# Two transformer blocks: seams between stages reordered, and a final sum shared between VectorE and TensorE

## The reference

```
h = modulate(rmsnorm(x), shift2, scale2)
group = top1 of softmax(h @ rg_w + rg_b)                # 4 groups
e_p, e_idx = top2 of softmax(h @ re_w + re_b)[group]    # 8 experts in a group
weights = g_p * e_p / sum(e_p)
y[token] += weight * ((silu(h @ w_gate[e]) * (h @ w_up[e])) @ w_down[e])
out = rmsnorm(x + gate2 * y, final_norm_g)
```

## Time and profile before

| | us |
|---|---|
| median of 3 runs | 3078.43 (3071.15 to 3080.0) |
| profiled execution | 3087.37 |
| its span, first to last instruction | 3085.6 |
| TensorE busy | 2895.9 (94%) |
| VectorE busy | 1779.8 (58%) |
| ScalarE busy | 1094.2 (35%) |
| mean granted TensorE clock | 0.970 |
| expert stage, its start to the next one's | 685.1 |
| last stage | 52.6 |

### The profile page before, as it was taken

One profiled execution on the slowest core, in us unless ns is written; L12 is line 12 of the kernel. 1 busy time (PEld: TensorE's weight loads), 2 busy tenths in 40 slices (PEclk: granted clock), 3 DMA queues, 4 the chain that ended last, 5 costly groups with the idle time before them and its releaser, 6 DMA issues. The chain is left out here.

```text
span 3085.6 us, 47695 instructions
## 1 busy us (share of the span) xinstructions
PE 2895.9 (94%) x19486; PEld 2179.9 (71%) x19486; DVE 1779.8 (58%) x2743; ACT 1094.2 (35%) x1700; POOL 454.5 (15%) x352
## 2 busy tenths in 40 slices
PE   8999999999999999989999999998898999999991
PEld 6877644676777777767747768687688777777760
DVE  3332222485566666555434626253874899999984
ACT  2111100122455454452231313222531566665652
POOL 2222100021322222213131101010000000000001
PEclk9999999999999999999999999998898999999995
DMA  4111031663222112121221211016346899999975
GB/s 167 45 38 45 15 129 55 184 194 123 61 61 63 55 55 62 56 100 51 68 56 34 65 29 60 7 59 202 129 166 224 329 396 397 398 398 398 397 286 231
DMA packets 290940, 454.44 MB, mean 147 GB/s; under 512 B 15760, under 2 KB 157584, under 8 KB 290752
## 3 DMA queue, kind: packets, MB, share of 16 engines
q1 hardware_dynamic: 283696, 426.06, 39.6%
q0 software_dynamic: 7056, 25.69, 2.1%
HBM read 389.77 MB, written 61.93 MB: 146 GB/s over the span
## 5 line engine op out<-in xcount | busy, mean ns | idle before, releaser
L1016 PE MATMUL psum<-x_hi,w_hi 128*128 128x512 f32 x512 | 210.6, 411 | 2.3 <-PEq L100 1.6
L1207 DVE TENSOR_TENSOR fox_pT_lo<-psum,fox_pT_hi 128x512 fp32r<-128x512 f32 (+2 forms) x192 | 107.1, 558 | 180.7 <-ACT fox_pT_hi L1146 171.6
L1018 PE MATMUL psum<-x_hi,w_lo 128*128 128x512 f32 x512 | 201.0, 393 | 0.0
L1017 PE MATMUL psum<-x_lo,w_hi 128*128 128x512 f32 x512 | 199.9, 390 | 0.0
L3065 ACT CAST hi_d<-land_d 128x2048 fp32r<-128x2048 f32 x66 | 122.8, 1909 | 141.0 <-PE psum L2935 141.0
L721 PE MATMUL psum<-wo,yT 128*128 128x512 f32 x384 | 167.6, 593 | 2.9 <-PEq L100 1.5
L1704 PE MATMUL psum<-hT,wr 128*128 128x512 f32 x384 | 167.1, 593 | 0.0
L3120 DVE TENSOR_TENSOR lo_d<-land_d,hi_d 128x2048 fp32r<-128x2048 f32 x66 | 148.3, 2289 | 21.5 <-ACT hi_d L3065 21.5
L3120 DVE TENSOR_TENSOR lo_g<-land_g,hi_g 128x2048 fp32r<-128x2048 f32 x66 | 150.6, 2283 | 0.1
L1157 ACT ACTIVATE fox_p<-fox_p,fox_bias 128x256 f32<-128x256 f32 (+7 forms) x128 | 99.6, 778 | 118.5 <-DVE fox_bias L1193 114.9
L180 PE MATMUL psum<-x_lo,w_hi 128*128 128x512 f32 x352 | 138.3, 393 | 0.0
(11 more groups left out here) (526 smaller groups left out, 7049.2 us busy)
## 6 DMA issues: line engine op xcount, KB each, us to landing
land_g<-in_moe_w_gate SPq DMA_DIRECT2D x66, 1024.0 KB, 7.9
land_u<-in_moe_w_up SPq DMA_DIRECT2D x66, 1024.0 KB, 8.9
land_d<-in_moe_w_down SPq DMA_DIRECT2D x66, 1024.0 KB, 9.4
ada<-in_ada_w SPq DMA_DIRECT2D x24, 1024.0 KB, 5.6
y_slots<-yb SPq DMA_DIRECT2D x33, 512.0 KB, 10.3
w<-in_w_in SPq DMA_DIRECT2D x27, 512.0 KB, 3.9
w_land<-in_w_kv_shared SPq DMA_DIRECT2D x23, 512.0 KB, 4.1
w_land<-in_w_in SPq DMA_DIRECT2D x23, 512.0 KB, 3.9
```

The lines of the kernel that those rows point to most:

```text
L1016: nc.tensor.matmul(bank[:], hi[:, d, :], E.x_hi[:, d, cols], start=(d == 0), stop=False)
L1017: nc.tensor.matmul(bank[:], hi[:, d, :], E.x_lo[:, d, cols], start=False, stop=False)
L1018: last = nc.tensor.matmul(bank[:], lo[:, d, :], E.x_hi[:, d, cols], start=False, stop=(d == ND - 1))
```

## The change

Stage by stage:

- *Constants*: the loads of `w0` move to SyncE of the next stage.
- *Output stages*: in the last tile TensorE runs all chunks of the left half, then all of the right one.
- *Attentions*: six fillers before the last head's transposes in the memory stage; six and twelve before those of the last two steps in fox.
- *Recurrent pairs*: VectorE's read of MT and N moves into `sums(c + 1)`, before its last two instructions; the ten fillers behind N go.
- *Mixing*: zeros are stored in turns 2 to 7, in six parts, not in turns 8 to 12. The router of tile 6 and nine fillers come before the last tile's transposes; its evacuation is shared between ScalarE and VectorE; eight plus eighteen fillers at the end become four.
- *Routing*: the ranks' sums become a scan over (expert, tile); the further blocks' offset is added once for all experts, and expert numbers come from the positions of the maxima; the table's matmuls are float32r and start on half of their input. `idx` comes before the splits of g0 and g1, the list of further blocks behind the first block's inputs. Block 0's inputs are prepared in two halves, the second by ScalarE. SyncE waits for the first gather before it loads expert 1.
- *Further blocks*: the number is loaded ahead of the last results; one `If(filled > 1)` stands around waits and loop; 24 fillers follow the last down projection.
- *Residual rows and final gain* are loaded in the last block of the experts, to a place that only routing tables and buffers of odd blocks used.
- *Last stage*: VectorE sums the left 512 columns; TensorE the right ones, as identity times residual plus two products with diagonal matrices of the weights, in PSUM. ScalarE squares both.

The core of the diff:

```diff
@@ stage_out, TensorE
-                    for c in range(NY):
+                    by_chunk = [(c, hf) for c in range(NY) for hf in range(2)]
+                    by_half = [(c, hf) for hf in range(2) for c in range(NY)]
+                    for c, hf in by_chunk if t < NT - 1 else by_half:
@@ stage_fox, TensorE
+                    if n >= STEPS - 2:
+                        keep_warm(nc, E, pe, ringP, 6 if n < STEPS - 1 else 12)
                     turn(n, 0)
@@ stage_memory_and_gates, TensorE
+                    else:
+                        keep_warm(nc, E, pe, ringD, 6)
                     attn.turn(pe, h)
@@ stage_rwkv_pairs
-                    if c + 1 < NPAIR:
-                        keep_warm(nc, E, pe, ringA, 10)
...
                     link(dve, V.tensor_tensor(bt[:], bt[:], e2[:], ALU.mult))
+                    if c >= 1:
+                        states(c - 1)
@@ stage_mix
+                    if t == NT + 3:
+                        router(t - 5)
+                        keep_warm(nc, E, pe, ringA, 9)
                     if 4 <= t <= NT + 3:
                         norm.turn(pe, t - 4)
-                    if 5 <= t:
+                    if 5 <= t and t != NT + 3:
                         router(t - 5)
                     out(t - 3, 1, 1)
-                    if t == NT + 3:
-                        keep_warm(nc, E, pe, ringD, 8)
-                keep_warm(nc, E, pe, ringD, 18)
+                keep_warm(nc, E, pe, ringD, 4)
...
-                    if t == NT:
+                    if t == 2:
                         sp.wait_ge(zeros_set, 1)
-                    if t >= NT:
+                    if t < 2 + ZERO_PARTS:
...
-                        norm.evacuate(act, t - 4)
+                        norm.evacuate(act, t - 4, halves=(0, 1) if t < NT + 3 else (0,))
...
+                    if t == NT + 3:
+                        last_rows_half()
@@ stage_experts
-            with eng.Fori(0, OVER - 1) as j:
-                with eng.If(filled > j + 1):
+            with eng.If(filled > 1):
+                begin()
+                with eng.Fori(0, OVER - 1) as j:
                     step(j)
...
+                sp.wait_ge(xg_in[0], 16)
                 for x in ("g0", "g1", "u0"):
                     load(x, 1)
...
+                    if isinstance(b, int) and b + 1 == LOOPED:
+                        sp.wait_ge(M["up_full"], LOOPED - 1)
+                        for t in range(NT):
+                            sp.dma_start(E.cx[t][:], x_rows[t * P:(t + 1) * P, :]).then_inc(E.cx_landed[t], 16)
...
-                pe.wait_ge(M["y_set"], LOOPED)
-                further_blocks(pe, further)
+                for _ in range(24):
+                    nc.tensor.matmul(gate_b[:, 0:P], E.ident[:], E.ident[:], start=True, stop=True)
+                further_blocks(pe, filled, lambda: pe.wait_ge(M["y_set"], LOOPED), further)
...
+                dve.wait_ge(R["table"], 1)
+                V.tensor_copy(idx[:], rank_b[:, 0:BLOCKS]).then_inc(R["idx"], 1)
                 lo("g0", 0)
                 lo("g1", 0)
-                dve.wait_ge(R["table"], 1)
-                V.tensor_copy(idx[:], rank_b[:, 0:BLOCKS]).then_inc(R["idx"], 1)
@@ stage_combine
+            @block.tensor
+            def _(pe):
+                right = slice(HALF, D)
+                def rows(t):
+                    pe.wait_ge(E.cx_landed[t], 16)
+                    nc.tensor.matmul(E.banks[t][:], E.ident[:], x[t][:, right], start=True, stop=False)
+                rows(0)
+                rows(1)
+                for t in range(NT):
+                    pe.wait_ge(y_in[0][t], 16)
+                    nc.tensor.matmul(E.banks[t][:], diag[0][t][:], y[0][t][:, right], start=False, stop=False)
+                    pe.wait_ge(y_in[1][t], 16)
+                    nc.tensor.matmul(E.banks[t][:], diag[1][t][:], y[1][t][:, right], start=False, stop=True).then_inc(half_summed, 1)
+                    if t + 2 < NT:
+                        rows(t + 2)
```

More of the change, by code:

```diff
@@ L320, in _ @@
                     nc.scalar.copy(E.mv[:, m, :], ring.bank(("v", m))[:])
+            @block.sync
+            def _(sp):
+                win = A["w_in"][0].rearrange("(c p) n -> p c n", p=P)
+                for i in range(2):
+                    col = (2 * (len(POOL_WINDOWS) - 1) + i) * P
+                    sp.dma_start(E.w0[i], win[:, :, col:col + P]).then_inc(E.w0_landed[i], 16)
             @block.gpsimd
@@ L641, in turn, with evacuate @@
             last.then_inc(ring.full, 1)
-    def evacuate(self, act, t):
+    def evacuate(self, act, t, halves=(0, 1)):
         nc, ring = self.nc, self.ring
-        for h in range(2):
+        for h in halves:
             act.wait_ge(ring.full, ring.nth(("t", t, h)))
@@ L2689, in weight_rests, with last_rows_half @@
                         V.tensor_tensor(w_o_lo[:, d, :], w_o[:, d, :], w_o_hi[:, d, :].bitcast(F32), ALU.subtract).then_inc(wo_split, 1)
+                def last_rows_half():
+                    t, h = NT - 1, 1
+                    dve.wait_ge(ringA.full, ringA.nth(("t", t, h)))
+                    for k in range(4):
+                        c = 4 * h + k
+                        last = V.tensor_scalar(norm.to[:, c, t * P:(t + 1) * P], ringA.bank(("t", t, h))[:, k * P:(k + 1) * P],
+                                               norm.scale[:, c:c + 1], norm.shift[:, c:c + 1], ALU.mult, ALU.add)
+                    last.then_inc(ringA.free, 1)
                 sq2 = sb("res_tmp", [P, HALF])
@@ L2765, in stage_experts @@
         yb = [sb(f"yb{i}", [P, D]) for i in range(2)]
[L2766 to L2768 removed]
+        at_part = [x[:] for x in x_hi]
+        before_r, ones_r = x_lo[0][:, 0, :], x_lo[0][:, 1, :]
+        keep = yb[0][:, 0:EXPERTS * NT]
+        tile_sums = yb[1][:, 0:EXPERTS * NT].rearrange("p (e t) -> p e t", t=NT)
+        passed = yb[1][:, EXPERTS * NT:EXPERTS * (NT + S // P - 1)].rearrange("p (e j) -> p e j", j=S // P - 1)
+        R = {x: E.sem("route_" + x) for x in ("consts", "gsub", "gexp", "ssub", "sexp", "both", "ranks", "places", "table", "idx", "over", "masks", "xm0", "xh0", "xl0", "xm1")}
         two = lambda name: [E.sem(f"{name}{i}") for i in range(2)]
```

320 lines of the change are left out of this document (177 added, 143 removed).

## The result

| | before | after |
|---|---|---|
| median, with the change | 3079.22 (4 runs, 3071.15 to 3081.94) | 3021.98 (4 runs, 3021.72 to 3028.91) |
| median, both once more | 3079.31 (21 runs) | 3020.63 (5 runs) |
| profiled executions | 3087.37 and 3081.7 | 3021.88 and 3024.0 |

What follows compares the result with a forecast made beforehand. TensorE, busy 94% of the 3085.6 us span, bounds the kernel, so gains come only from its waits, lower clock and fillers at seams. Terms sum to -70 us: 3017 from the profile, 3008 from the median; 8-in-10 range 2995 to 3023.

Steps and rivals of the forecast that it cites:

- each gain is a shift of all that follows: All seams: each ends in a barrier or feeds an engine without slack, so the gains add up, -70 us.
- Start, -3.0: First barrier: SyncE no longer holds it with the w0 loads, next stage begins earlier; -3.0 us, bounds 0 and 3.5.
- Output stages, -2.8: Last tile of two output stages: first half's additions and statistics lie beside TensorE's second half; -1.4 us twice.
- Attentions: Ends of the memory stage and forgetting attention: fillers shorten waits and keep TensorE's clock full; -3.3 and -5 us.
- Recurrent pairs, -7.3: Three seams of the pairs: VectorE reads the bank earlier and TensorE's fillers go; -2.4 us each.
- End of mixing, -12.5 with the zeros: Last tile of mixing: router and fillers fill TensorE's wait, clock holds, -13.5 us; zeros stored earlier cost 1.
- Routing and first block, -13.6: Expert stage's start: idx at 23.4 us, first matmul at 31.7 against 47.0; -13.6 us remain, bounds -9 and -15.3.
- VectorE is late next: First expert block: VectorE's block list and weights reach into the next modulation, leaving 13.6 of 15.3 us.
- The whole stage moves with its first matmul: Expert loop of 33 blocks: TensorE sets the period, unchanged at 18.5 us, so the earlier start carries through.
- Further blocks, -9.1: Behind the last expert block: register read earlier, one branch replaces 14 skipped passes; -9.1 us, bounds -10.5 and -7.
- Last stage, -13.5: Final stage: early residual rows and TensorE's share of sums cut 52.6 us to 39.1; bounds 36 and 53.
- four rivals: TensorE at 1.2 GHz in last stage (3022, 0.14); 398 GB/s bound (3019, 0.08); slower loop (3090, 0.02); upper bounds (2995, 0.10).

Runs made afterwards that it cites:

- before_pairs: Kernel before with only the recurrent pairs' change (VectorE's read moved earlier, ten fillers removed): 3079.6 us, ratio 0.9997.
- the moved instruction: Changed kernel with VectorE forming the first block's hidden values before, not behind, the split of block 1's second gate piece: 3017.6 us, ratio 0.9792.
- after_no_pairs: Changed kernel with the recurrent pairs' part undone (ten fillers back, states read late): 3030.4 us, ratio 0.9834.

## Why the prediction was right and where it was not

Nearly all causes were right, and the sum was 13 us too large. The step that failed is "each gain is a shift of all that follows", together with carrying the sum over to the median. At three places something else took part of the gain back: waits for issue in the pairs (4.8 us left of 7.3), a slower gather, the lower clock and a longer period in the experts (19.8 of 22.7), and the transfers in the last stage (11.8 of 13.5). The stages gave 61.7 us instead of 70.1, and the median 57.2.

- **Start, -3.0.** Right in its cause; the means gave -4.4, beyond the 3.5 that the bounds named, 1.5 of it since TensorE's clock is full from the first matmul of the next stage. In the first profile of after it did not show, because the rows landed late.
- **Output stages, -2.8.** Measured -0.6 and -1.6; the second stage takes 160.6 in the two kernels with the order of before whose pairs were changed, behind it in the program, and 162.0 in the others; why was not looked into.
- **Attentions.** The memory stage gave 3.5 for 3.3 by the means; single profiles of the changed kernel and its variants lie between 185.6 and 191.5. The forgetting attention gave 3.4 for 5: the clock was full in the last six us as forecast, but the fillers of the step before delay what stands behind them by 0.6, and the last step still waits 1.1 and 1.1 us.
- **Recurrent pairs, -7.3.** The mechanism was right: 2.1 to 2.5 at each of three seams for the 2.4 forecast, and VectorE has time to spare behind (it now waits 7.75). The stage gave 4.8. The step that failed is the silent one, that all else in the stage stays as it is: TensorE waits for issue at other places, which differ by up to 7 us between kernels with the same order.
- **End of mixing, -12.5 with the zeros.** Measured -11.3. "The router 1.8" was 2.94 and the four fillers 2.05 instead of 0.9, because the clock fell again. The stores of zeros cost nothing that shows. Part of the gain hung on the clock of before: in the three profiles with other code ahead of it the old order took 221.3 to 222.6 instead of 226, its last fillers running at the higher clock (4.26 us in before_pairs instead of 6.88). That the position does this, and not chance, three profiles do not show.
- **Routing and first block, -13.6.** Idx came 0.4 behind the forecast, and between 23.4 and 24.9 over the profiles of the changed kernel and its variants. "The gather then has the queues alone", "I take 4.6 us", failed: 6.2 pass, as GpSimd is 2.93 us in the issue (1.33 before) although the landing then takes 3.2. The rows' transposes ran at the lower clock (1.97 us instead of 1.04), which no term named, and the first matmul followed 4.6 behind the landing instead of 3.4 (3.5 in the second profile, at the full clock). It came at 34.9 of the stage instead of 31.7. And "VectorE is late next" was right, but was priced by its wait alone; the clock lost behind that wait costs up to 2 more, as the moved instruction shows. Measured, by the first block's results, 10.5 to 12.8.
- **The 33 blocks, no term.** "The whole stage moves with its first matmul" and "its period unchanged at 18.5" failed by little: 18.43 and 18.61 in turn instead of 18.46, 1.8 us in the loop, most of what the experts' two terms were too large by.
- **Further blocks, -9.1.** From the start of VectorE's last result to the barrier 15.76 became 6.47: 9.3. The fillers are late next as said, by 0.9.
- **Last stage, -13.5.** Measured -11.8. That VectorE's time per tile sets the end was right for the kernel before and wrong for the changed one: there the last gather, landing at 32.3, and 8.1 behind it make 40.4. The transfers were called near, and they were the bound. Two terms were small: the first pair landed at 7.3, not 6.6, and VectorE's instructions of half width took 0.75, not 0.69. The terms as written (6.6 + 0.7 + 4.5 + 20.65 + 3.7 + 3.6) also make 39.75, not 39. That the number is so near is partly luck, since both bounds lie at about 40.
- **The median.** Carrying the difference of one profile over to the runs' median took the profile's 70 us as 70 of the median. 5.6 us of that profile's 3087.4 were chance in two stages, which no term described. The first profiles differ by 65.5, the medians by 57 to 59.

So of the miss of 14 us, 8.4 are terms: experts 2.9, pairs 2.5, last stage 1.7, forgetting attention 1.6, mixing 1.2 and output stages 0.6 too large, the start 1.4 and small things 0.6 too small. 4.5 are what the medians' difference (57.2) lies below the sum of the stages' means (61.7). The intervals of the two ratios are 49 to 61 us and 57 to 66 us, and no run resolves that rest further. With the variants counted that the table leaves out, the stages' sum is 59.7 and 2.5 of the rest remain; which set is the more typical is open.

None of the four rivals happened. The first was the nearest in its number (3022), and not by its mechanism: the clock came up to 0.88 in the last stage, and where it was 0.79 the stage took 41.5 us against 40.8 on average.

## What to carry to other kernels

Take two profiles of the kernel before when the forecast is carried to a median, and compare them stage by stage: what differs between them belongs in no term. In a stage of short matmuls, judge an edit over several positions of the code, because one pair of kernels shows the edit plus where the stalls for issue happened to fall. Full queues do not say what ends a stage: look for the engine's last wait. In the last stage they were full for some 39 us before the change, and VectorE ended it; after it they were full for 32, and they ended it. Work out both bounds, since a cut in one is worth only what the other leaves. And where a loop is said to stay as it is, compare its period to the hundredth: 0.06 us a block were 1.8 in all.

## What the runs showed of the hardware

- Moving TensorE's code, with nothing in it changed, puts waits for issue of up to 1.8 us at new places in the same stage and takes others away, of up to 3 us. All of those looked at lie in or behind groups of 64 x 64 matmuls, whose 64 records take 1.16 us. The one at L1760 was there in all ten executions with that position, 1.4 us long in three and 2.6 to 3.1 in seven by the weight loads' rows, and behind the long one of the first profile the next matmuls ran at the lower clock. Instructions come by a DMA queue of their own, in packets of 16 KB; the stage of pairs draws 64 of the 140 in the kernel (DMA view of that stage):
```profile
q8 instruction: 64, 1.05, 0.8%
```
  The Trainium skill ("Runtime: NRT & Kernel Launch", Instruction fetch mechanics) says the same of the 16 KB blocks and calls the cost of passing from one to the next mostly hidden. In this stage it is not: 1.5 us three times in after_no_pairs, 3 us at once in after. The traces tie the waits to these packets. In the 18 profiles the stage of pairs has 25 waits of TensorE for issue of 0.9 us or more, and each ends 1.1 to 1.7 us behind the end of an instruction packet, of which one comes in 9 us on average. At L1760 in after TensorE stands still from 352.2 to 355.1 us of the stage, and the packet runs from 352.6 to 353.5; in the three executions with the short wait it starts 1.25 to 1.3 ahead of the wait. So TensorE waits for instructions that come late; why they are late at one place and not at another was not shown.
- The first gather of the expert stage took GpSimd 2.93 to 3.12 us to issue (2.23 where another had gone ahead), the same instruction mostly 0.94 later in the stage, and 1.33 in the kernel before, where the queues were busy with weights at that moment.
- TensorE's clock fell behind a wait of 1.46 us at the end of mixing and held behind one of 1.44 between two groups of transposes in the first stage of the second profile, while it fell behind 1.94 at the same place in the first. A filler group ahead of a wait does not by itself keep the clock behind it.
